# Long convolutions: filter sizes summed by channel inside the projection, filter weights scaled and summed instead of filters, the inverse transform issued two chunks late

## What is computed

```
def hyena_mixer(h, w_in, b_in, conv_w, conv_b, f_*, filt_bias, w_out):
    x1, x2, v = split(short_conv(h @ w_in + b_in, conv_w, conv_b))
    filt = MLP with three sine layers of width 64, then @ f_w4, times decay;
           filt /= sum over positions of |filt| + eps      (per channel, order and direction)
    z = v
    for o, gate in enumerate((x1, x2)):
        z = gate * bidir_long_conv(z, filt[:, o, 0], filt[:, o, 1], filt_bias[o])
    return z @ w_out
```

## Time and profile before

| | |
|---|---|
| median of 3 runs | 3289.98 us (3283.84 to 3293.68) |
| profiled execution, its time | 3287.9 us |
| its span | 3286.1 us |
| TensorE busy | 3008.9 us (92%) |
| VectorE busy | 2076.2 us (63%) |
| ScalarE, GpSimd busy | 1257.2 us, 416.5 us |
| projection (`phase_hyena_in`) | 670.2 to 833.4 us |
| long convolutions | 833.8 to 1145.6 us |

### The profile page before, as it was taken

One profiled execution on the slowest core, in us unless ns is written; L12 is line 12 of the kernel. 1 busy time (PEld: TensorE's weight loads), 2 busy tenths in 40 slices (PEclk: granted clock), 3 DMA queues, 4 the chain that ended last, 5 costly groups with the idle time before them and its releaser, 6 DMA issues. The chain is left out here.

```text
span 3286.1 us, 32817 instructions
## 1 busy us (share of the span) xinstructions
PE 3008.9 (92%) x12672; PEld 2352.3 (72%) x12672; DVE 2076.2 (63%) x2409; ACT 1257.2 (38%) x1480; POOL 416.5 (13%) x125
## 2 busy tenths in 40 slices
PE   6897889979788789998999998999989999989998
PEld 5435766758666657777777876888868777778887
DVE  7676799778788737997456744566036566456631
ACT  4442477632111135875222233444132222344422
POOL 0201000024000010000000000344400000024442
PEclk8898899989888889999999998999989999999999
DMA  6244499722000014994322222222222222222222
GB/s 238 71 135 179 173 412 396 273 80 101 24 16 17 21 65 170 361 359 166 122 77 72 95 90 77 97 95 102 90 109 90 77 77 90 90 89 90 102 92 82
DMA packets 91293, 424.12 MB, mean 129 GB/s; under 512 B 10231, under 2 KB 15479, under 8 KB 64920
## 3 DMA queue, kind: packets, MB, share of 16 engines
q1 hardware_dynamic: 87704, 397.12, 33.5%
q10 hardware_dynamic: 3456, 25.17, 1.9%
HBM read 420.15 MB, written 2.10 MB: 128 GB/s over the span
## 5 line engine op out<-in xcount | busy, mean ns | idle before, releaser
L220 PE MATMUL psum<-h_high,weights_low 128*128 128x512 f32 x1856 | 735.7, 396 | 21.7 <-DVE h_low L339 8.6
L221 PE MATMUL psum<-h_high,weights_high 128*128 128x512 f32 x1856 | 729.9, 393 | 0.0
L222 PE MATMUL psum<-h_low,weights_high 128*128 128x512 f32 x1856 | 729.4, 393 | 0.0
L183 POOL TENSOR_TENSOR weights_low<-weights_raw,weights_high 128x2048 fp32r<-128x2048 f32 x84 | 392.2, 4669 | 2282.2 <-ACT weights_high L179 2282.2
L179 ACT ACTIVATE weights_high<-weights_raw 128x2048 fp32r<-128x2048 f32 x166 | 317.8, 1914 | 803.0 <-PE psum L222 769.4
L220 PEld LDWEIGHTS psum<-h_high,weights_low 128*128 128x128 f32 x1856 | 353.2, 190 | 107.4 <-issue 32.3
L221 PEld LDWEIGHTS psum<-h_high,weights_high 128*128 128x128 f32 x1856 | 353.3, 190 | 74.5 <-issue 1.4
L222 PEld LDWEIGHTS psum<-h_low,weights_high 128*128 128x128 f32 x1856 | 352.9, 190 | 74.6
L339 DVE TENSOR_TENSOR weights_low<-weights_raw,weights_high 128x2048 fp32r<-128x2048 f32 x82 | 187.9, 2293 | 316.7 <-ACT weights_high L179 316.7
L1579 DVE TENSOR_TENSOR weights_low<-more_raw,weights_high 128x1024 fp32r<-128x1024 f32 x168 | 203.3, 1223 | 16.6 <-ACT weights_high L1198 9.6
L2594 DVE SCALAR_TENSOR_TENSOR ff_tiles<-psum,params,ff_tiles 128x510 f32<-128x510 f32 (+1 forms) x176 | 123.7, 745 | 135.1 <-ACT ff_tiles L2572 129.1
(11 more groups left out here) (431 smaller groups left out, 4828.7 us busy)
## 6 DMA issues: line engine op xcount, KB each, us to landing
weights_raw<-in_moe SPq DMA_DIRECT2D x168, 512.0 KB, 5.6
more_raw<-in_moe SPq DMA_DIRECT2D x168, 512.0 KB, 5.6
weights_raw<-in_w_mix SPq DMA_DIRECT2D x76, 1024.0 KB, 4.9
weights_raw<-in_w_ffn SPq DMA_DIRECT2D x66, 1024.0 KB, 4.9
mod_weights<-in_ada_w ACTq DMA_DIRECT2D x24, 1024.0 KB, 8.0
mod_weights<-in_ada_w SPq DMA_DIRECT2D x32, 512.0 KB, 3.6
weights_raw<-in_hy_w_in SPq DMA_DIRECT2D x12, 1024.0 KB, 4.9
mod_weights<-in_ada_w SPq DMA_DIRECT2D x8, 1024.0 KB, 22.5
```

Of the source, the lines that this page charges most:

```text
L183: self.nc.gpsimd.tensor_tensor(self.low[:, g % 2, :], self.raw[:, g % 2, :], self.high[:, g % 2, :].bitcast(F32), ALU.subtract).then_inc(s ...
L220: nc.tensor.matmul(out, w[1], rhs[0], start=start, stop=False)
L221: nc.tensor.matmul(out, w[0], rhs[0], start=False, stop=False)
L222: return nc.tensor.matmul(out, w[0], rhs[1], start=False, stop=stop)
```

## The change

**In the projection.** The filter network's hidden values are made in 128 rows, twice the same 64 (the weights are laid out twice by the host). A high and a low part of them are kept (`hidden_high`, `hidden_low`). From unit 4 on, four "size tiles" are put into each unit on TensorE, after its 2nd, 6th, 10th and 14th group: two fp32r products of 128x512 (L1709, L1710) give 128 filters by channel, with positions along the row. ScalarE takes their absolute values (L1756), and VectorE multiplies by the decay, laid out by channel, and sums along the row in one instruction (L1832, `tensor_tensor_reduce`), which gives each channel's size. That is 32 tiles. SP loads a decay table of 2 MB into the rows of `x_x_v` that are written last, and eight pieces of `hy_f_w4` of 256 KB; each piece is split into high (ScalarE) and low (VectorE, 64 rows). Units use three pairs of PSUM banks instead of four. The units' low parts stay on GpSimd. The wait for the third sine argument moves from ahead of unit 3 to the first size tile.

**In the long convolutions.** The inverted sizes scale the last layer's weights (L2036, 128x256), and sum and difference are taken of the weights (L2038, L2039), not of the filters. TensorE flips them (L1895), ScalarE rounds them (`weights_high`), VectorE makes the low part, and TensorE makes the already scaled sum and difference filters from fp32r products of 128x256 (L1922, L1923, 20 a chunk), which VectorE multiplies by the decay (L2053). Absolute values, their sums, the ones product, the inversion of 128x512, the scaling and the sum and difference of 128x1024 are gone. z and its spectrum have banks 0 to 3, the filter spectrum and the inverse banks 4 to 7, and the weights' flip bank 6. The inverse of chunk i - 2 is issued in the round of chunk i, and the filters of chunk i + 1 are made in the same round.

The diff, cut to its core (new lines of the size tiles, then of the convolutions):

```diff
+            def size_tile(p, q):
+                x, at = 4 * p + q, slice(q * P, q * P + P)
+                if x == 0:
+                    pe.wait_ge(s.arg, 3)
+                    pe.wait_ge(s.hidden_low, 1)
+                if q == 0:
+                    pe.wait_ge(s.w4_low, p + 1)
+                if x >= 2:
+                    pe.wait_ge(s.absed, x - 1)
+                out = m.psum[:, 6 + x % 2, :]
+                nc.tensor.matmul(out, stack[:, p % 2, at], m.hidden_high[:, :], start=True, stop=False)
+                nc.tensor.matmul(out, stack[0:FILTER_WIDTH, p % 2, at], m.hidden_low[0:FILTER_WIDTH, :],
+                                 start=False, stop=True).then_inc(s.tiles, 1)
...
+                    if u >= lag and i % 4 == 1:
+                        size_tile(u - lag, i // 4)
...
+                if u >= lag:
+                    for x in range(4 * (u - lag), 4 * (u - lag) + 4):
+                        act.wait_ge(s.tiles, x + 1)
+                        if x >= 4:
+                            act.wait_ge(s.normed, x - 3)
+                        nc.scalar.activation(sizes[:, x % 4, :], m.psum[:, 6 + x % 2, :], ACT.Abs).then_inc(s.absed, 1)
...
+                        nc.vector.tensor_tensor_reduce(out=size, in0=size, in1=decay[:, p, :], scale=1.0, scalar=0.0,
+                                                       op0=ALU.mult, op1=ALU.add, accum_out=m.sizes[:, x:x + 1])\
+                            .then_inc(s.normed, 1)
...
-            for i in range(chunks + 1):
-                if i < chunks:
-                    filters(i)
+            for i in range(chunks):
+                if i:
                     z_spectrum(i)
-                if i:
-                    inverse(i - 1)
-                if i < chunks:
-                    filter_spectrum(i)
+                    pe.wait_ge(s.k_done, 2 * i)
+                else:
+                    pe.wait_ge(s.filtered, 2)
+                if i + 1 < chunks:
+                    flip_weights(i + 1)
+                if i >= 2:
+                    inverse(i - 2, 4)
+                if i + 1 < chunks:
+                    flip_z(i + 1)
+                    pe.wait_ge(s.w_low, i + 2)
+                    filters(i + 1, 0, Z[:, 4:8, :])
+                if i >= 2:
+                    pe.wait_ge(s.gated, 2 * (i - 1))
+                transform(K, 0, As[i % 2][:, 0, :, :], s.k_sums)
+                if i + 1 < chunks:
+                    pe.wait_ge(s.z_out, i + 2)
+                    filters(i + 1, 1, Z[:, 0:4, :])
+                transform(K, 1, As[i % 2][:, 1, :, :], s.k_sums)
+            pe.wait_ge(s.k_done, 2 * chunks)
+            inverse(chunks - 2, 4)
+            inverse(chunks - 1, 0)
...
+            for i in range(chunks):
+                if i:
+                    for which in range(2):
+                        butterflies(i - 1, K, Ks[(i - 1) % 2], which, s.k_odd, s.k_done)
+                    multiply(i - 1)
+                    for which in range(2):
+                        butterflies(i, Z, F, which, s.u_odd, s.u_done)
+                if i + 1 < chunks:
+                    weights_low(i + 1)
+                if i >= 2:
+                    gate(i - 2, 4)
+                if i:
+                    spectrum_pairs(i - 1)
+                if i + 2 < chunks:
+                    weight_sums(i + 2)
+                if i + 1 < chunks:
+                    filter_decay(i + 1, 0, Z[:, 4:8, :])
+                    filter_decay(i + 1, 1, Z[:, 0:4, :])
```

More of the change, by code:

```diff
@@ L1663, in _ @@
             nc.gpsimd.memset(U[:, :, :, :], 0.0).then_inc(s.pads, 1)
-            ring.make_lows(pool, n)
+            for _ in range(n):
+                ring._make_low(pool, ring.lowered)
+                ring.lowered += 1
         @block.tensor
@@ new lines, in _ @@
+            for u in range(n):
+                if u >= 3:
+                    pe.wait_ge(s.read_out, u - 2)
+                w = [x.rearrange("p (k m) -> p k m", k=KC) for x in ring.parts(pe, u)]
+                for i in range(2 * KC):
+                    j, k = (i % 2, i // 2) if u == 0 else (i // KC, i % KC)
+                    if u == 0 and j == 0:
+                        h_ready(k)
+                    mm = split_matmul(nc, m.psum[:, banks(u)[j], :], [x[:, k, j * P:(j + 1) * P] for x in w],
+                                      [x[:, k, :] for x in m.Hs], k == 0, k == KC - 1)
+                    if u >= lag and i % 4 == 1:
+                        size_tile(u - lag, i // 4)
+                mm.then_inc(ring.used, 1)
@@ new lines, in transform @@
+            def transform(out, which, src, done):
+                for parity in range(2):
+                    for kt in range(2):
+                        for c in range(2):
+                            j = 2 * parity + c
+                            mm = nc.tensor.matmul(out[:, 4 * parity + 2 * which + kt, :],
+                                                  m.fwd[:, which, j, kt * P:(kt + 1) * P], src[:, j, :],
+                                                  start=(c == 0), stop=(c == 1))
+                mm.then_inc(done, 1)
@@ new lines, in gate @@
+                    tt(m.xv[:, 16 + t, :], gated, m.xv[:, 8 * order + t, :], ALU.mult).then_inc(s.gated, 1)
+                    dve.wait_ge(s.gated, 2 * i + c + 1)
+            link(nc.vector.tensor_scalar(m.sizes[:, :], m.sizes[:, :], EPS, None, ALU.add))
+            link(nc.vector.reciprocal(m.sizes[:, :], m.sizes[:, :]))
+            weight_sums(0)
+            weight_sums(1)
+            for which in range(2):
+                butterflies(0, Z, F, which, s.u_odd, s.u_done)
+            weights_low(0)
@@ L1982 @@
+            last = chunks - 1
+            for which in range(2):
+                butterflies(last, K, Ks[last % 2], which, s.k_odd, s.k_done)
+            multiply(last)
+            spectrum_pairs(last)
+            gate(last - 1, 4)
+            gate(last, 0)
 RAW_Q, RAW_K, RAW_G, RAW_SC, RAW_SX, RAW_CA, RAW_CB = 0, 2, 4, 8, 12, 16, 20
```

447 lines of the change are left out of this document (248 added, 199 removed).

## The result

The changed kernel takes **3270.27 us**, median of 6 runs (3267.48 to 3276.05); the kernel before, timed beside it, takes 3289.59 us. The ratio is 0.9943, 95% interval 0.9929 to 0.9957: faster by 0.57%, 19 us. The forecast was 3219, with a range of 3204 to 3246. The sign was right and the size was not: 51 us of the expected gain are missing.

The account below looks back on a forecast made before the run. TensorE was taken to bound the projection and, after the change, the long convolutions. 14.5 + 0.8 - 84.7 = -69.4 us from the profiled 3287.9 gave 3218.5, forecast as 3219, range 3204 to 3246.

Parts of the forecast that it names:

- What bounds: TensorE bounds the projection now and becomes the long convolutions' bound, at 25.3 us a round against VectorE's 22.4.
- Size tiles on TensorE: Projection: 64 added products at 0.2263 us, 14.5 us all on the path; a unit goes from 10.86 to 12.67 us.
- Long convolutions, TensorE: Transforms, flips and 20 filter products at 0.12 us (0.113 to 0.19) sum to a round of 25.3 us, 24.9 to 26.9.
- The clock: Start of the long convolutions: TensorE begins at the lower clock, for which 4 us were added.
- Start and end: Long convolutions: 21.6 us to the first filter transform, rounds, tail 27.7; 223 in all, 227 with the clock.
- Does TensorE stay fed?: Long convolutions: VectorE's loop of 16.2 us fits TensorE's 17.0 with 0.8 us to spare, through the inverse two chunks late.
- VectorE in the projection: Four reductions and a low part bring a unit to 12.4 to 12.7 us against TensorE's 12.67; cost taken as 0.
- The estimate of 12.9 us a unit by the lock: Projection: VectorE's new work can hardly run beside GpSimd on the shared port; the end slips by up to 2 us.
- The rivals: TensorE waits every round, 3241, 13%; VectorE bounds projection, 3257, 7%; full clock not granted, 3431, 3%; order fails, 3269, 2%.
- the order does not do what it says: Long convolutions: each round keeps TensorE's 6.4 us of waits, 31.7 us a round, +50, 3269; chance 2%.
- rounds over 27 us: Long convolutions: named beforehand as a sign of being wrong; rounds of 25.3 us were expected.
- -2 at unit 4: Projection: lower bound on the shift from unit 4's changed start, taken as +0.8 us with bounds -2 and +4.

Follow-up runs that it names:

- e1_full_rows: Changed kernel with both low products (size tiles and filters) on all 128 rows in place of 64; 3222.02 us, ratio to before 0.9802.
- e8_vector_4: Full rows in both low products, plus four more VectorE instructions of 128x512 in every round behind the complex product; 3236.40 us, one run.
- e2_full_rows_sizes_only: Changed kernel with all 128 rows for the low product of the size tiles alone, filters still alternating; 3258.01 us, one run.
- e4_all_half_rows: Changed kernel with the high products of size tiles and filters on 64 rows too; 3244.75 us, one run.
- e5_turned: Changed kernel, row counts kept, every second token tile taking its low filter products first so equal row counts are neighbours; 3243.2 us, one run.
- e9_kept_busy: Full rows in both low products, plus throwaway TensorE products where it idled at the start of the long convolutions; 3216.28 us, ratio 0.9781.

## Why the prediction was wrong

**What bounds.** Right: TensorE is the bound in both stages, and VectorE's work in a round is 21.7 us against 21.8 to 22.4.

**Size tiles on TensorE: 64 x 0.2263 = 14.5 us.** This step failed first. It took every product at the pace of its like, one after another, and had no term for neighbours that differ. With equal rows (e1_full_rows) a unit is 12.9 us and the next stage starts at 849.8, against 12.67 and 849; as changed it is 14.6 and 862.8. The missing term is 64 changes x 0.21 = 13 us. Of the 0.2 us between 12.67 and 12.9, the ordinary products' pace of 0.231 in place of 0.2263, no run here shows the cause.

**Long convolutions, TensorE: 20 fp32r products of 128x256 at 0.12, at most 0.19.** This step failed by most. The value 0.12 was exact for products of equal rows, and wrong for these, which alternate: 0.31. 160 changes x 0.194 = 31 us. The upper bound was no bound: it was set from one row of 128-row products under "each weight load waited for", and called a little above it. The longest spacing that a load and a product in series could give had to be worked out from both, and the estimate of 0.22 from the Trainium skill (TensorE: Matmul & The Clock Gate, "LDWEIGHTS"), a round of 27.2, which stood beside it, was nearer but still under the measured 28.3.

**What I looked at and did not read.** I wrote that the 64-row halves cost as much as full ones, which is right for each alone. The earlier trace rows has 64-row products only sixteen in a row, but the trace of the kernel before shows changes elsewhere, even in the projection: the filter network's 64-row products stand between the projection's. TensorE's timeline there, then the weight loads:

```profile
699.52 1.07 PE L1678 MATMUL psum<-filter_hidden,w 64*64 64x512 f32 x2 [0.89 <-ACT filter_hidden L1704]
700.52 0.50 PE L220 MATMUL psum<-h_high,weights_low 128*128 128x512 f32 x1
700.85 0.39 PE L221 MATMUL psum<-h_high,weights_high 128*128 128x512 f32 x1
...
700.51 0.19 PEld L220 LDWEIGHTS psum<-h_high,weights_low 128*128 128x128 f32 x1 [0.81 <-issue]
700.62 0.19 PEld L221 LDWEIGHTS psum<-h_high,weights_high 128*128 128x128 f32 x1
```

Behind the 64-row products the load of L220 begins with its product, and L221 starts 0.33 us later, where 0.23 is ordinary: the same picture as at a size tile. (These products also have 64 columns of weights in place of 128; further on in that trace, at 1681.62 us, L220 follows products of 64 rows and 128 columns, and its neighbour starts 0.34 us later.) The sign was there before the change, and with it a price could have been estimated. The change's diff shows the alternation plainly, in one pair of lines. An arrangement that none of the rows read covered should have been a rival with a price of its own.

**The clock.** I gave it 4 us, at the start only. The changed kernel's long convolutions are 38.7 us longer than those of e1_full_rows; 31 are the changes at the full clock's price, and the other 8 are put down to the lower clock: in the start, where a change costs more (at a granted clock of 0.50 a filter product took 0.51 us, against 0.21 in e1_full_rows), and in half transforms of 5.41 us, one of 6.14 us behind the wait of 4.55. Why the stream with the gaps gets less clock is open. That it does rests on five traces: slow half transforms without a wait before them in the two whose filters alternate throughout, none, once the first rounds are past, in the three with 0 to 8 changes a round.

**Start and end: 21.6 us, rounds 22.7, 25.4, 24.1, tail 27.7, and 4 for the clock.** In e1_full_rows: 27.3, then 24.06 with a wait of 4.56 us for the z butterflies (L2062) that I had not seen, rounds of 24.4 where I had 25.4, and 228.2 in all against 227. The rounds were summed from durations where starts were meant: a transform takes 7.07 us but the next product starts 6.91 after it, and the flips 0.79 and 0.43, not 1.09 and 0.55. The parts were off by a few us each and cancelled, so the 227 came out by luck; with TensorE kept busy the start is 21.6, as summed.

**Does TensorE stay fed?** Right in every middle round, by less than I thought: on e1_full_rows 0.3 to 0.4 us of slack, not 0.8 (e8_vector_4). That the lag does it is shown: one round less costs 41 us. I had said that no wait for L2091 or L2053 would stand; there is one of each, 1.64 us in the last round and 1.32 in the start, besides the 4.55 for L2062.

**VectorE in the projection** costs nothing, right: the reductions (L1832) have a median of 689 ns, and in e1_full_rows TensorE is busy all of 88.0 us with VectorE at 82.8. The estimate of 12.9 us a unit by the lock that the Trainium skill states (SBUF — State Buffer, "SBUF: two separate sides") is what e1_full_rows took, but not by the lock, since TensorE never waited.

**The rivals and the range.** None of the rivals came true; of the signs of being wrong, rounds over 27 us did. The time is near the 3269 of "the order does not do what it says", by accident: the inverse moved, and the waits of 6.4 us in a round are gone. The low end of the range did not follow from its terms either: filters at 0.113, no loss of clock at the start and -2 at unit 4 take about 8 us off 3219, which is 3211 and not 3204; and the forecast left out the 2.1 us between the profiled execution and the median that it named.

**The sum.** With the two terms that were missing, 13 and 31, and 8 for the clock, 3219 becomes 3271. Measured: 3270.3. Without changes of row count (e1_full_rows): 3222.0 against 3219. That both fit within 3 us is in part luck, since small errors cancel, among them the 4 us that the rest of the program took less and the 2.1 us left out.

## What to carry to other kernels

Sum a TensorE stream by the distance between starts, in the order in which its products stand, and look at what each product's neighbour is: here each change between 64 and 128 rows cost 0.2 us, more than the whole of a 256-column product. Where some products need fewer rows, fill them to the full count, or group them so that equal ones are neighbours; here a harmless term in the extra rows cost no time (zeros were not tried). And a TensorE that is "busy" throughout may still be standing: the weight loads (PEld) that begin together with their product, not before it, show it.

## What the runs showed of the hardware that I had not expected

- A change of row count between neighbouring products cost 0.19 us (256 columns) to 0.21 us (512 columns) at a granted clock of 1.00 and 0.30 us at 0.50 (0.51 against 0.21 a product in the start). Products of 64 rows among themselves take 0.12 us, as those of 128 do.
- Streams in which the row count alternates, with products 0.31 us apart and no wait, had half transforms of 5.41 us in place of 3.72 in some rounds: two in the changed kernel, three in e2_full_rows_sizes_only (granted clock 0.98 over 154 us and 0.97 over 160 us without a wait), none, once the first rounds were past, in e1_full_rows, e4_all_half_rows and e5_turned (1.00 over 136 to 141 us).
- The same short waits were followed by either clock. Behind a wait of 2.0 us an inverse took 8.86 us in the changed kernel and 7.18 in e1_full_rows; behind 2.7 us one took 8.82 us in e1_full_rows, 10.20 in e9_kept_busy and 7.17 in e5_turned.
